# SwiGLU gate and up of a two-layer diffusion backbone: seven block products for each pair of chunks instead of eight

## The reference, cut to what matters

```python
def swiglu(x, w_up, w_down):
    gate, up = jnp.split(x @ w_up, 2, -1)
    return (jax.nn.silu(gate) * up) @ w_down

for i in range(DEPTH):                      # 2 layers, D_MODEL 1024, D_FF 2816, fp32
    h = h + 0.5 * ml[2] * swiglu(modulate(h, norm_g[i, 0], ml[0], ml[1]), ffn_w_up[i, 0], ffn_w_down[i, 0])
    ...   # the same for hc (256 context tokens)
    h = h + ml[5] * y                       # y: the layer's mixer
    h = h + 0.5 * ml[8] * swiglu(modulate(h, norm_g[i, 2], ml[6], ml[7]), ffn_w_up[i, 1], ffn_w_down[i, 1])
```

## Time and profile before

| | |
|---|---|
| median of 3 runs | 3035.66 us (3035.28 to 3035.75) |
| the profiled execution | span 3035.1 us, from the first to the last instruction |
| mean granted TensorE clock | 0.995 of full speed |
| busy share | TensorE 97%, weight loads 92%, VectorE 52%, GpSimd 33%, ScalarE 31% |
| four SwiGLU stretches | 540.9, 559.0, 550.5 and 369.8 us |
| the mixer of layer 0 and its projections | 600.7 to 1266.8 us |
| the mixer of layer 1 and its projections | 2381.6 to 2652.0 us |

### The profile page before, as it was taken

How to read it: one execution, slowest core, us unless ns; L and a number is a source line. 1 busy time by engine, 2 the same in 40 slices (tenths; PEclk the granted TensorE clock), 3 DMA queues, 4 the chain that set the end, 5 groups by cost and what they waited for, 6 DMA issues and landing times.

```text
span 3035.1 us, 45968 instructions
## 1 busy us (share of the span) xinstructions
PE 2956.5 (97%) x19039; PEld 2782.4 (92%) x19039; DVE 1576.7 (52%) x2456; ACT 945.1 (31%) x1645; POOL 999.0 (33%) x557
## 2 busy tenths in 40 slices
PE   8999999999999989999999999999999998999998
PEld 8999999899888877999999999999999877798997
DVE  7556666894646665667677683212123356421222
ACT  4212212353454455321121232212123236532222
POOL 1333333323322214233333333222222234444443
PEclk9999999999999999999999999999999999999999
DMA  6334454223320032234434332121211210232232
GB/s 251 118 120 137 126 141 137 95 72 119 112 67 11 8 98 75 99 124 132 139 126 144 130 101 70 63 63 59 67 59 53 76 48 2 71 97 94 89 95 71
DMA packets 126380, 285.31 MB, mean 94 GB/s; under 512 B 40238, under 2 KB 57566, under 8 KB 126046
## 3 DMA queue, kind: packets, MB, share of 16 engines
q1 hardware_dynamic: 123438, 275.97, 28.4%
q10 hardware_dynamic: 2736, 6.40, 0.5%
HBM read 270.73 MB, written 15.10 MB: 94 GB/s over the span
## 4 chain that ended last, share of the span: by engine, by line
PE 90%; DVE 4%; ACT 3%; issue 1%; DMA 1%; POOL 0%; SPq 0%; ACTq 0%; POOLq 0%; DVEq 0%
PE psum L1869 80%; PE psum L2043 2%; PE psum L2126 1%; DVE o_acc L1702 1%; PE psum L2149 1%; PE psum L2136 1%; PE psum L2028 1%; PE psum L2084 1%; PE psum L2063 1%; DVE prob_o L1803 1%; PE psum L2050 1%; PE psum L1891 0%; PE psum L2009 0%; ACT probT_o L1318 0%; PE psum L2026 0%
## 5 line engine op out<-in xcount | busy, mean ns | idle before, releaser
L944 POOL TENSOR_TENSOR wl<-raw,wh 128x1024 fp32r<-128x1024 f32 (+1 forms) x326 | 831.6, 2551 | 1685.2 <-ACT wh L1034 1684.0
L1869 PE MATMUL psum<-uh,wh 128*128 128x256 f32 (+5 forms) x2704 | 660.9, 326 | 7.7 <-POOL wl L944 4.1
L1869 PE MATMUL psum<-uh,wl 128*128 128x256 f32 (+5 forms) x2704 | 657.1, 324 | 0.0
L1869 PE MATMUL psum<-ul,wh 128*128 128x256 f32 (+5 forms) x2704 | 656.7, 324 | 0.0
L1869 PE MATMUL psum<-ah,wh 128*128 128x386 f32 (+4 forms) x2192 | 596.3, 344 | 5.9 <-POOL wl L944 5.9
L1869 PE MATMUL psum<-ah,wl 128*128 128x386 f32 (+4 forms) x2192 | 591.5, 342 | 0.0
L1869 PE MATMUL psum<-al,wh 128*128 128x386 f32 (+4 forms) x2192 | 589.7, 341 | 0.0
L1596 DVE SCALAR_TENSOR_TENSOR ada_product<-ada_w,cb 128x1024 f32<-128x1024 f32 x256 | 478.3, 1868 | 5.1
L1869 PEld LDWEIGHTS psum<-uh,wh 128*128 128x128 f32 (+1 forms) x2704 | 450.7, 189 | 30.7 <-issue 8.8
L1869 PEld LDWEIGHTS psum<-ul,wh 128*128 128x128 f32 (+1 forms) x2704 | 451.0, 189 | 19.1
L1869 PEld LDWEIGHTS psum<-uh,wl 128*128 128x128 f32 (+1 forms) x2704 | 448.7, 189 | 19.8
(11 more groups left out here) (262 smaller groups left out, 2372.2 us busy)
## 6 DMA issues: line engine op xcount, KB each, us to landing
raw<-in_w SPq DMA_DIRECT2D x264, 512.0 KB, 3.7
ada_w<-in_ada_w SPq DMA_DIRECT2D x128, 512.0 KB, 3.8
raw<-in_w SPq DMA_DIRECT2D x64, 448.0 KB, 3.5
spill<-cacc ACTq DMA_DIRECT2D x16, 384.0 KB, 2.6
scale_w<-in_scale_w SPq DMA_DIRECT2D x8, 512.0 KB, 14.8
ada_w<-bias_final SPq DMA_DIRECT2D x16, 256.0 KB, 3.1
ada_start<-in_ada_w SPq DMA_DIRECT2D x7, 512.0 KB, 15.8
h<-in_xT SPq DMA_DIRECT2D x8, 384.0 KB, 15.3
```

What stands on the lines that cost most here:

```text
L944: nc.gpsimd.tensor_tensor(wl[n % SPLIT_SLOTS][:, 0:k * w], raw[n % RAW_SLOTS][:, 0:k * w], wh[n % SPLIT_SLOTS][:, 0:k * w].bitcast(f32), A ...
L1869: ins = nc.tensor.matmul(pair[0:w, lo:hi], wt[n % SPLIT_SLOTS][:, k * w:(k + 1) * w], xt[:, k, cols], start=first, stop=last)
```

## The change

The first four pairs of each SwiGLU stay as they are. For the other 18, gate and up over the two halves of the 1024 input features are a 2 x 2 block matrix of quarters (A11, A12: gate; A21, A22: up; each four weight tiles, 512 columns), and the token tile is a 2 x 2 block matrix too: rows are the halves of the features, columns the halves of the tokens. Their product is made from seven block products instead of eight. Each is an item of 4 x 3 = 12 matmuls of 386 or 384 columns: P1 (A11) and P2 (A12, first token columns), P3 (A12 - S2), P4 (A22), P5 (A21 + A22), P6 (S2 = A22 - (A11 - A21)) and P7 (A11 - A21). In the list a pair j is P6, P7, P5, P1 of j+1, P4, P3, P2 of j+1.

- GpSimd makes the four sums of quarters in place in `raw` and in `held` (`quarter_sum`); VectorE makes the low parts of the seven quarters (`pair_lows`), ScalarE the high ones (`split_unit`), in a ring of six halves, up to four items ahead. The weights of `down` and of the first four pairs keep GpSimd for their low parts.
- P6 is added on top of P1, P5 on top of P6 and P3 on top of P5 in one PSUM bank, P4 on top of P7 in bank 3. ScalarE copies P1, P6 and P5 into `held` before the next is added (`hold_product`); VectorE adds these copies to P2, P7 and P4 (`pair_product`) and multiplies with `rstd`. P4's matmuls wait for `quarter_added`, VectorE's sum of the copy of P5 and of P7's bank (`released`).
- The sums of token tiles (T1, T2, T4 for P5, P6, P4, and T3 in place for P7) are made once for each SwiGLU by ScalarE, GpSimd and VectorE beside the first four pairs and the first downs (`t_make`, `t_sums`, `t_highs`, `t_lows`, `t3_*`).
- `PARTS = [4, 2, 4, 4, 4, 4]`: 48 downs for each SwiGLU instead of 24, with four or two weight tiles each. `sg` and `af` lie in one buffer each. `ada_plan` gives the chunks by shares. The first two downs of a part are interleaved (`first_downs`) and wait for the last result only at their last weight tile.
- Semaphores are merged and some buffers moved, without an effect on the order outside the SwiGLUs.

```diff
-PARTS = [8, 7, 7]
+PARTS = [4, 2, 4, 4, 4, 4]
+CLASSIC = 4
...
+            if j == CLASSIC:
+                items += [("P1",) + key, ("P2",) + key]
+            items += [("P6",) + key, ("P7",) + key, ("P5",) + key]
+            after = [(kind,) + chunks[j + 1] for kind in ("P1", "P2")] if j + 1 < FFC else []
+            items += after[:1] + [("P4",) + key, ("P3",) + key] + after[1:]
...
+    def shares(x):
+        if x[0] == "down":
+            return 1 if x[3] < 2 else 2
+        return {"gate": 2, "up": 2, "P7": 1, "P1": 1, "P2": 1}.get(x[0], 0)
...
+            if kind in PAIR:
+                q = pair_no[x[1:]]
+                return [{"P1": (held_copied, 3 * q + 1), "P6": (held_copied, 3 * q + 2), "P5": (held_copied, 3 * q + 3),
+                         "P2": (quarter_added, 3 * q + 1), "P7": (quarter_added, 3 * q + 2), "P4": (quarter_added, 3 * q + 3),
+                         "P3": (pair_scaled, 3 * q + 3)}[kind]]
...
+            elif kind in PAIR:
+                place[x] = ({"P2": 2, "P7": 3, "P4": 3}.get(kind, x[5] % 2), 1)
...
+        def unit_ahead(x):
+            return 4 if x[0] in PAIR or x[0] == "down" else 2
...
+                elif x[0] == "P7":
+                    for kind in ("gate", "up"):
+                        r, m, _ = raw_place[slot_of[(kind,) + x[1:]]]
+                        pool.wait_ge(raw_loaded[r], 16 * m)
+                    pool.wait_ge(pair_lo, pair_low_no[("P1",) + x[1:]] + 1)
+                    if q:
+                        pool.wait_ge(summed, 4 * q)
+                    nc.gpsimd.tensor_tensor(a11, a11, a21, ALU.subtract).then_inc(summed, 1)
...
             for x in items:
                 i = number[x]
-                split_up_to(sum(number[y] <= i + 2 for y, _, _ in slots))
+                split_up_to(i)
+                if i and items[i - 1][0] == "P3":
+                    glu_high(items[i - 1])
+                if x[0] in ("P1", "P6", "P5"):
+                    hold_product(x)
+                elif x[0] == "P3":
+                    pair_silu(x)
...
+                elif x[0] == "P5":
+                    dve.wait_ge(held_copied, 3 * q + 3)
+                    dve.wait_ge(a_lo, g)
+                    nc.vector.tensor_tensor(af[:, tail], u4[:, 0:narrow], product("P7", second), ALU.add).then_inc(quarter_added, 1)
...
+                for k in range(HALF_K):
+                    xh, xl = pair_moving(x, k)
+                    tile = slice(P * k, P * k + P)
+                    for wt, xt, first, last in ((high, xh, fresh and k == 0, False), (high, xl, False, False),
+                                                (low, xh, False, k == HALF_K - 1)):
+                        ins = nc.tensor.matmul(bank, wt[:, tile], xt, start=first, stop=last, skip_group_check=not fresh)
```

More of the change, by code:

```diff
@@ L498, in build @@
                 place[x] = (4, 2)
+            elif kind in PAIR:
+                place[x] = ({"P2": 2, "P7": 3, "P4": 3}.get(kind, x[5] % 2), 1)
+            elif kind == "down":
+                place[x] = (4 + 2 * (x[4] % 2), 2)
+                turn = 0
             elif kind in ("vt", "start"):
@@ new lines, in t_tiles, with pair_moving @@
+        def t_tiles(x, j):
+            high, low = a_of(x)
+            first, second = (width_of(cols) for cols in halves(x))
+            t1_at, t2_at = NARROW * j, HALF_K * NARROW + WIDE * j
+            flat = [t[:, HALF_K:KD, :].rearrange("p a b -> p (a b)") for t in (high, low)]
+            return [[f[:, t1_at:t1_at + second], f[:, t2_at:t2_at + first], t[:, j, 0:first]] for f, t in zip(flat, t4)]
+        def pair_moving(x, k):
+            if x[0] in ("P5", "P6", "P4"):
+                return [t[{"P5": 0, "P6": 1, "P4": 2}[x[0]]] for t in t_tiles(x, k)]
+            row = {"P1": k, "P2": HALF_K + k, "P3": HALF_K + k, "P7": k}[x[0]]
+            return [t[:, row, columns_of(x)] for t in u_of(x)]
@@ L954, in _ @@
             for x in items:
-                split_up_to(sum(number[y] <= number[x] + 2 for y, _, _ in slots))
+                split_up_to(number[x])
+                for j in T_SUMS.get(x, []):
+                    t_sums(x, j)
+                if x[0] == "down" and x[3] == 0 and x[4] < HALF_K:
+                    t3_sums(x, x[4])
                 if x == ("spread",):
@@ L1881, in dense, with first_downs @@
                 return ins
+            def first_downs(x, second):
+                first = glu_no[next(y for y in items if y[0] in ("up", "P3") and y[1:4] == x[1:4])[1:]]
+                last = PARTS[x[3]] - 1
+                for y in before[second]:
+                    for signal in released(y):
+                        pe.wait_ge(*signal)
+                for y in (x, second):
+                    pe.wait_ge(lo_split, low_no[y] + 1)
+                    for k in range(last):
+                        if y == x:
+                            pe.wait_ge(a_lo, first + k + 1)
+                        dense_step(y, k, *a_of(y))
+                pe.wait_ge(a_lo, first + last + 1)
             def start_scale(k):
@@ L1965, in _ @@
                         ready = lambda k: pe.wait_ge(late_lo, KD * late_no[m] + k + 1)
-                    if x[0] == "down" and x[4] == 0:
-                        first = glu_no[next(y for y in items if y[0] == "up" and y[1:4] == x[1:4])[1:]]
-                        ready = lambda k: pe.wait_ge(a_lo, first + k + 1)
                     if x[0] == "out" and x[2] == 0:
```

503 lines of the change are left out of this document (393 added, 110 removed).

## The result

3218.6 us (median; 3215.7 to 3222.5) against 3035.5 us beside it on the same chip: ratio **1.060** (95% interval 1.059 to 1.062), slower by 183 us. The forecast said 3083 us and gave 3145 as its upper end: the side was right, the size a quarter of what came.

The account below looks back on a forecast made before the run. TensorE, 97% busy, was taken as the bound: 3035.1 less 140.2 us of matmuls gives a floor of 2894.9; 187 us of VectorE and GpSimd waits in the four stages bring 3082, forecast 3083 us, range 2992 to 3145.

Parts of the forecast that it names:

- The pair walk: One new pair followed through the engines' queues in stage C: period 16.85 us, 2.0 over TensorE's 14.82; D 14.3 us.
- A, B and D: SwiGLU stages: layer 0 first, layer 0 second, layer 1 second (latent columns only); forecast 561, 588 and 386 us long.
- burst loops: Pair loops with three GpSimd sums in a row, 8 a stage; forecast over floor: C 2.0, D 4.2, A 4.6, B 5.6 us each.
- C: SwiGLU stage, layer 1 first, without adaLN work; forecast 532 us long, 20 us over the floor.
- about 12 us late: A's first part: VectorE's 45.8 us of work, 57 with waits and collisions, against five products of 42 us.
- 5 at changes of part: Stage A: 5 us lost at changes of part, within its 58 us over the floor.
- 12; 2 more: Stage B: 12 us for downs with a chunk, update of h, GpSimd low and next pair's lows; 2 us more; total 67.
- 4 for first pairs: Stage D: 4 us for first pairs of parts, whose release of P4, due at 5.8 us, comes later under the burst.
- The 96 extra updates of h ... I cost at nothing in C and D: Updates of 1.14 us each, claimed covered by TensorE's 8.5 us a classic product; without cover up to 20 us a stage.
- Rival 2: Pauses in burst loops of A, B and D also drop TensorE's clock: up to 41 us more, 3124 us; chance 0.16.
- Rivals 1 and 4: 1: TensorE stays bound, 2978 us, chance 0.22; 4: stages C, D pay for A, B, 3036 us, 0.06.
- Rival 3: Full serialisation: every GpSimd sum adds its whole length to VectorE's queue, plain loops too: 3190 us; chance 0.06.

Follow-up runs that it names:

- experiment 11: The change with adaLN chunks beside the first four pairs and the downs cut to 64 of 1024 columns, those beside new pairs whole: 3132.8 us.
- experiments 9 and 10: Both against the change. 9: same adaLN chunks, none beside the new pairs, 3254.1 us. 10: 24 of B's 72 chunks moved to C's downs, 3188.9 us.
- experiments 2 and 13: Both against the change. 2: GpSimd's quarter sums 64 columns in C and D, 3184.1 us. 13: ScalarE's silu and result earlier at part ends, 3226.6 us.
- experiments 6 to 8: 6: new pairs in C alone, 3037.1 us. 7: also VectorE's changed order, 3026.7. 8: also edits beside the pairs undone in A, B, D, 3014.9.

## Why the prediction was wrong

- *Matmuls, floor*: right. 216 fewer a stage, and where nothing waits a pair takes 14.7 us (14.8 forecast).
- *The pair walk*: right in its total, in part by luck. VectorE idles 1.7 us for P1's high part, and the sums and VectorE's operations hold each other up, as the walk had it; P4 waits for L1755 behind VectorE's queue in A, B and D. But P4's pauses are 1.8 us in the burst loops of D and mostly 2.6 in those of A and B, not 3 to 5, and in C only 0.17; there P5's wait for ScalarE's copy of P6 (0.60) is longer, and the prediction had counted such a wait as a sign of being wrong. The walk is 0.75 us too long in C's burst loops and 1.2 in D's (14.3, measured 13.1), and the stretches at half clock, which it left out, fill part of that again: 138 us for 148 forecast. The upper bound of the sum is off as well: it adds 44 for the rest, where its own terms give 38.
- *Stages*: C 18 us shorter as forecast, but by luck: 16.5 and 3 were forecast for its loops and its rest, 10.1 and 10.0 came. A, B and D 69, 87 and 42 longer where 20, 29 and 16 were forecast.
- **The step that failed** is "about 12 us late" and "5 at changes of part" in A, "12; 2 more" in B, "4 for first pairs" in D: 38 us, measured 182. In A and B it is mis-sized, not misplaced: with the chunks beside downs and first pairs short, 35 and 55 us of it go (experiment 11). A's four changes of part cost 15 us more than C's, where 5 stood in the sum; B's start, changes and end cost 13, 35 and 13 us more than C's, where 14 stood in the sum for all of them. I compared a down's 4.23 us with 4.2 of VectorE's and called that nearly even. But the next pair's lows (0.6 each) stand in the same queue, the adaLN products take 1.53 us in the mean (L1966, 390.7 us in 256), not the 1.26 of the sum, because GpSimd's operations hold some of them up, and the backlog is met by the next P4 (6.12 us). The kernel before showed that the 1.26 was too low:

```profile
L1596 DVE SCALAR_TENSOR_TENSOR ada_product<-ada_w,cb 128x1024 f32<-128x1024 f32 x256 | 478.3, 1868 | 5.1
```

There the same product takes 1.87 us in the mean; the sum took the time of one that nothing holds up. A queue that is filled to 100% has no room for collisions; each chunk more or less there is worth 2.2 to 2.6 us, about its full length (experiments 9 and 10).

- *"The 96 extra updates of h ... I cost at nothing in C and D"*: in C nearly right (10 us), in D wrong, where the rest is 38.5 us and not 4. What holds it stays open: that a ring of two weight buffers does not keep up with D's downs of 2.8 us is argued from the rows, and experiments 2 and 13 show only that neither GpSimd's sums (32 us stay) nor ScalarE's order is it. I read the cover of 8.5 us from the pairs before, not from the short downs of the change; the prediction said itself what it would cost if the cover went (up to 20 us a stage).
- *Rival 2, the clock*: its sign showed up in the records (150 us at half clock in A, B and D), and in single loops its price too (1.1 to 1.6 us, with 1.7 forecast as the most); in the total it gave 7 us for a third of it, which leaves the miss of 136 us almost whole.
- *Rivals 1 and 4*: out. *Rival 3* was out in kind (loops are not serialised whole), though its 3190 us came nearer than my forecast.
- *Edits costed at nothing outside the new pairs* (single buffers for gate and up, downs in two pairs of banks): 14 us in three stages without new pairs (experiments 6 to 8).
- *"A granted clock under 1 in the pair stretches ... means rival 2"* was a bad test: the clock was low in A, B and D while most of the loss was elsewhere.

## What to carry to other kernels

Before moving work to an engine that is busy half of the time, add up its queue in each short phase (start, change of part, end), not only in the main loop. Where it comes out within a few per cent of the bound engine's time, nearly every microsecond more is paid. And take an operation's length from its mean over the kernel before, collisions included, not from one that ran undisturbed. A saving of matmuls is best taken only where the helpers have room: in one stage of four this one was worth 0.7%, once VectorE's order and the edits beside the pairs were mended (0.0% as it was); in all four, as built, it cost 6%. And the order of a queue can be half of the loss, as it was in C: work that frees a buffer goes ahead of work that is only needed four items later.
